# Router logits with the router stationary, routing regrouped, clearing moved to GpSimd, and two stage ends replaced by single waits

## The chip, the cores and the metric

One core of one Trainium2 chip runs the whole program as a single launch. The metric is the device time of one execution in microseconds (us); the number compared is the median of the runs. The engines are TensorE (PE, with its weight loads listed apart as PEld), VectorE (DVE), ScalarE (ACT), GpSimd (POOL) and SyncE (SP), whose queue issues the large transfers.

## What is computed

A trunk of two layers works on 256 latent tokens and 256 context tokens of width 1024. Each layer mixes tokens (attention and a recurrent scan), projects, adds the result, normalises again and applies a channel mixer. The change lies in the second layer, whose channel mixer is a mixture of experts on the 256 latent tokens:

```python
def moe_swiglu(h, router, w1, w3, w2):
    logits = jnp.einsum('bld,de->ble', h, router, preferred_element_type=F32)
    top_v, top_i = lax.top_k(logits, TOP_K)          # TOP_K = 2 of N_EXPERTS = 8
    wts = jax.nn.softmax(top_v, axis=-1)
    gates = jnp.sum(jax.nn.one_hot(top_i, N_EXPERTS, dtype=F32) * wts[..., None], axis=-2)
    y = jnp.zeros_like(h)
    for e in range(N_EXPERTS):
        y = y + gates[..., e:e + 1].astype(h.dtype) * swiglu(h, w1[e], w3[e], w2[e])
    return y
```

## The kernel before

Everything is float32; large products are made from two bf16 parts each (a high part and the rest). Tokens lie in tiles of 128, tiles 2 and 3 being the latent ones; the width is 8 blocks of 128 (`KC`).

**Order of the work.** Every engine has its own program, written out by hand. Engines hand work to one another through semaphores, and at the end of each stage all four compute engines drain and wait for each other (`stage_end`, L394 to L399). The second layer's stages are: mix, levels, states, out (the output projection and the residual add), then one stage with the norm and the routing, one short stage with the first gather, the expert loop, and a last stage that adds the result.

**Norm (L498 to L588).** ACT squares the rows, POOL forms the inverse root, DVE scales the rows into `XN`, PE turns 16 blocks (L583) into PSUM banks, and DVE (L566) and ACT (L535) take them in turn, modulated, into `HT`.

**Routing (L1455 to L1530).** PE computes the logits token-stationary: for each of 2 token tiles and 8 blocks the 128x128 tokens are the weights and the 8 router columns stream (L1458, 16 products, two instructions each as all float32 products here). Then it turns the 16 normalised blocks back into rows (L1463). DVE ranks the 8 logits of each token in a chain of dependent small instructions (L1486 to L1497, ended by the semaphore `r_sel`), computes the gates (L1499 to L1506), waits for PE's five position products (L1469 to L1473), computes positions and the number of rounds (L1509 to L1517), forms the low bf16 part of the rows (L1521, four instructions) behind ACT's high part (L1530), and clears `Y` and `PT` (L1522, L1523). A stage end follows.

**First gather.** PE clears two PSUM banks with products on the zeroed `PT` (L1621, 8 instructions), waits for the one-hot matrix of DVE (L1708), gathers expert 0's tokens (L1605, 32 products); ACT and DVE take them (L1697, L1703). A second stage end follows.

**Experts.** The 24 weight pieces of an expert (16 of 1408 KB, six of 1536 KB, two of 1024 KB) go through a ring of 8 slots. SP issues a piece when its slot is free (L1568, L1580), DVE splits it (L1754), PE multiplies it (L1633 to L1636, L1655). Pieces 0 to 5 of expert 0 are issued ahead, as soon as the states stage is over; pieces 6 and 7 when PE begins the first gather's stage (`pe.sem_inc(S("m_used"), NSLOT - EARLY)`); piece 8 when PE is through with piece 0.

## Time and profile before

| | us |
|---|---|
| median of 3 runs | 1955.58 |
| lowest, highest | 1955.06, 1958.46 |
| span of the profiled execution (the page gives no other time of it) | 1958.8 |
| its stretch from the first turned block of the second layer's second norm to the first weight split | 1225.4 to 1258.0 |
| its stretch from there to the end of the span | 1258.0 to 1958.8 |

The profile has a page of sums and slices, and answers on single stretches: who waited for whom, the chain of work that ended last, instructions in order of time, and the busy share of each engine in a stretch. Times in it are counted from the first instruction. The granted clock is that of TensorE as a share of full speed: 1.00 is 2.4 GHz and 0.50 is 1.2 GHz. A mean duration of a pipelined product includes its overlap with the next; the busy time of a group divided by its count is what one costs in a row.

### The profile page before, as it was taken

How to read it: one execution, taken by the hardware profiler on the slowest of the kernel's cores; microseconds unless marked ns; L12 is line 12 of the kernel's file. 1: busy time of each engine (PE TensorE's matmuls, PEld its weight loads, DVE VectorE, ACT ScalarE, POOL GpSimd, SP SyncE). 2: the span in 40 equal slices, each digit the busy share in tenths (PEclk: the TensorE clock that was granted, in tenths of full speed). 3: DMA queues.
4: the chain of work that ended last, by engine and by line, in shares of the span. 5: the costliest groups of instructions: out<-in, count | busy, mean ns of one | idle time of the engine just before them, and what ended most of it. 6: DMA issues, size and time to landing. Idle time of an engine off the chain costs nothing.

```text
span 1958.8 us, 33901 instructions
## 1 busy us (share of the span) xinstructions
PE 1774.0 (91%) x14848; PEld 1120.0 (57%) x14891; DVE 1169.3 (60%) x1387; ACT 371.3 (19%) x669; POOL 79.2 (4%) x68
## 2 busy tenths in 40 slices
PE   4999999978799999998999966799999998989996
PEld 2334556664344434444556643687786877768683
DVE  2021166874422323223234585699999999999996
ACT  2001055222422212211013323201010010001000
POOL 0032000020000000000230001000000000000000
PEclk9989999999899999999999998699999999999998
DMA  9731200002454544230222105299999999999998
GB/s 332 306 129 65 83 4 25 19 1 86 150 195 179 208 151 178 101 88 20 86 71 80 44 1 220 104 401 407 410 413 412 411 413 409 402 403 413 402 411 349
DMA packets 114969, 420.24 MB, mean 215 GB/s; under 512 B 14008, under 2 KB 20856, under 8 KB 108688
## 3 DMA queue, kind: packets, MB, share of 16 engines
q1 hardware_dynamic: 112784, 417.13, 54.7%
q8 instruction: 118, 1.93, 0.4%
q10 hardware_dynamic: 2048, 1.02, 0.3%
q14 instruction: 19, 0.16, 0.0%
HBM read 417.08 MB, written 1.05 MB: 213 GB/s over the span
## 4 chain that ended last, share of the span: by engine, by line
PE 68%; DVE 17%; DMA 7%; issue 4%; ACT 2%; DVEq 1%; POOL 1%; SPq 0%; POOLq 0%; PEldq 0%; ACTq 0%; PEld 0%
PE PS L1346 11%; PE PS L1655 11%; PE PS L618 10%; DVE ARENA L1754 8%; PE PS L616 8%; PE PS L1306 6%; DMA ARENA<-in_moe_w 6%; PE PS L1241 3%; PE PS L445 2%; PE PS L1633 2%; PE PS L1636 2%; PE PS L1635 2%; PE PS L1134 2%; DVE ARENA L801 1%; DMA ARENA<-in_ada_w 1%
## 5 line engine op out<-in xcount | busy, mean ns | idle before, releaser
L1754 DVE TENSOR_TENSOR ARENA<-ARENA 128x2816 bf16<-128x2816 f32 (+1 forms) x192 | 583.5, 3084 | 19.0 <-DMA ARENA<-in_moe_w 16.7
L1633 PE MATMUL PS<-ARENA 128*128 128x96 bf16 x2816 | 368.2, 207 | 29.9 <-DVE ARENA L1754 26.3
L1636 PE MATMUL PS<-ARENA 128*128 128x96 bf16 x2816 | 367.8, 207 | 2.6 <-issue 2.5
L1635 PE MATMUL PS<-ARENA 128*128 128x96 bf16 x2816 | 367.8, 207 | 0.5 <-issue 0.5
L1633 PEld LDWEIGHTS PS<-ARENA 128*128 128x128 bf16 x2816 | 276.9, 98 | 37.6 <-DVE ARENA L1754 30.1
L1635 PEld LDWEIGHTS PS<-ARENA 128*128 128x128 bf16 x2816 | 277.0, 98 | 9.4 <-issue 8.4
L1636 PEld LDWEIGHTS PS<-ARENA 128*128 128x128 bf16 x2816 | 276.9, 98 | 2.6 <-issue 2.4
L618 PE MATMUL PS<-ARENA 128*128 128x512 f32 (+1 forms) x608 | 243.0, 540 | 0.0
L1655 PE MATMUL PS<-ARENA 128*96 128x512 bf16 x1056 | 237.5, 384 | 2.8 <-DVE ARENA L1754 2.8
L1346 PE MATMUL PS<-ARENA 128*128 128x512 bf16 x1030 | 234.2, 385 | 4.4 <-DVE ARENA L1377 2.8
L378 DVE TENSOR_TENSOR ARENA<-ARENA 128x4096 bf16<-128x4096 f32 (+1 forms) x26 | 91.4, 3522 | 202.1 <-ACT ARENA L372 202.0
L1655 PEld LDWEIGHTS PS<-ARENA 128*96 128x96 bf16 x1056 | 127.9, 122 | 106.2 <-issue 3.9
L1346 PEld LDWEIGHTS PS<-ARENA 128*128 128x128 bf16 x1056 | 103.2, 99 | 139.7 <-issue 20.1
L618 PEld LDWEIGHTS PS<-ARENA 128*128 128x128 f32 x608 | 111.2, 194 | 87.0 <-issue 81.5
L616 PE MATMUL PS<-ARENA 128*128 128x512 f32 (+1 forms) x384 | 156.3, 567 | 0.0
L616 PEld LDWEIGHTS PS<-ARENA 128*128 128x128 f32 x384 | 73.6, 193 | 83.1 <-issue 80.7
L1306 PE MATMUL PS<-ARENA 128*128 128x512 bf16 x517 | 113.5, 379 | 1.5 <-DVE ARENA L1402 0.9
L679 DVE COPY ARENA<-PS 128x512 f32<-128x512 f32 (+1 forms) x24 | 13.4, 558 | 145.7 <-PE PS L618 145.7
L372 ACT ACTIVATE ARENA<-ARENA 128x4096 bf16<-128x4096 f32 (+1 forms) x26 | 74.9, 2888 | 108.3 <-PE PS L1306 68.3
L1306 PEld LDWEIGHTS PS<-ARENA 128*128 128x128 bf16 x528 | 51.6, 98 | 63.5 <-issue 1.4
L1718 ACT ACTIVATE ARENA<-PS 128x384 f32<-128x384 f32 (+1 forms) x48 | 20.7, 464 | 274.5 <-PE PS L1636 274.2
L1241 PE MATMUL PS<-ARENA 128*128 128x512 bf16 x282 | 63.2, 385 | 3.2 <-DVE ARENA L1266 3.0
(224 smaller groups left out, 1603.0 us busy)
## 6 DMA issues: line engine op xcount, KB each, us to landing
ARENA<-in_moe_w SPq DMA_DIRECT2D x136, 1408.0 KB, 16.6
ARENA<-in_moe_w SPq DMA_DIRECT2D x48, 1536.0 KB, 21.0
ARENA<-in_ada_w SPq DMA_DIRECT2D x24, 2048.0 KB, 10.1
ARENA<-in_ffn_w SPq DMA_DIRECT2D x15, 2048.0 KB, 7.9
ARENA<-in_w_in SPq DMA_DIRECT2D x12, 2048.0 KB, 8.0
ARENA<-in_moe_w SPq DMA_DIRECT2D x16, 1024.0 KB, 18.6
ARENA<-in_w_out SPq DMA_DIRECT2D x8, 1024.0 KB, 5.5
ARENA<-in_w_in SPq DMA_DIRECT2D x4, 1024.0 KB, 6.4
```

The costliest lines, as they stand in the source:

```text
L372: act.activation(it["hi"], raw, ACT.Copy).then_inc(S("split_hi"), 1)
L378: dve.tensor_tensor(it["lo"], it["raw"], it["hi"], ALU.subtract).then_inc(S("split_lo"), 1)
L616: mm = pe.matmul(B(bank)[:, part], slot[:, k, P * u:P * u + P], HT[:, k, part], start=k == 0, stop=k == KC - 1)
L618: mm = pe.matmul(B(bank)[:, part], HT[:, k, P * u:P * u + P], slot[:, k, part], start=k == 0, stop=k == KC - 1)
L1241: mm = pe.matmul(B(len(ts) * h + i), a[:, k, P * x:P * x + P], b[:, j, :], start=k == 0 and m == 0, stop=k == KC - 1 and m == 2)
L1306: mm = pe.matmul(B(2 * x + h), a[:, c, P * x:P * x + P], w[:, at:at + 512], start=c == 0 and n == 0, stop=c == FC - 1 and n == 2)
L1346: mm = pe.matmul(B(b0 + i % 3), w[:, k, P * c:P * c + P], x[:, k, :], start=k == 0 and w is hi and x is HTH, stop=k == KC - 1 and w is lo)
L1633: pe.matmul(out, hi[:, f:f + P], HEH[:, k, :], start=k == 0 and b % 4 == 0, stop=False, skip_group_check=True)
L1635: pe.matmul(out, hi[:, f:f + P], HEL[:, k, :], start=False, stop=False, skip_group_check=True)
L1636: mm = pe.matmul(out, lo[:, f:f + P], HEH[:, k, :], start=False, stop=k == KC - 1, skip_group_check=True)
L1655: mm = pe.matmul(B(YBANK + h)[0:SLOTS, :], x, y[:, at:at + 512], start=c == 0 and n == 0, stop=c == FC - 1 and n == 2)
L1754: dve.tensor_tensor(WLO[q % NSLOT][:, 0:n], RAW[q % NSLOT][:, 0:n], WHI[q % NSLOT][:, 0:n], ALU.subtract).then_inc(S("m_lo"), 1)
```

## The change

- The normalised blocks of this norm go to a place of their own (`HTR`), so that slots 6 and 7 of the ring (which lie over `HT`) can be filled early: piece 6 waits for the last product of the output projection, and piece 7 goes out behind it.
- The logits are computed router-stationary: the router's 8 columns are the weights and all 256 tokens stream, 8 products in place of 16, placed between the turned blocks of the norm. The result is 8x256, so DVE copies it and PE turns it twice, back to tokens by experts.
- The rows are turned behind the logits in four groups, each with its own semaphore step, and ACT and DVE take them group by group.
- DVE's chain is reordered: ranking, two low parts, positions of the first round, one-hot, two low parts, other positions, number of rounds, and only then the gates.
- PE gathers as soon as the low parts are done. The clearing of `PT` and `Y` goes from DVE to POOL, at the end of the states stage; PE's zero products (now two, in bf16) stand ahead of the norm's turned blocks.
- The stage ends behind the routing and behind the first gather are gone; the semaphores `m_pt`, `r_rounds` and `m_cleared` are waited for instead.

```diff
+        HTR = A(150, KC, 256)
+        LGT = A(158.5, 256)
...
         def pe_route(pe):
+            def logits(k):
+                pe.wait_ge(S(n + ("ht_act" if k % 2 else "ht_dve")), 24 + k // 2 + 1)
+                return pe.matmul(B(LBANK)[0:N_EXP, 0:256], ROUT[:, k, :], HTR[:, k, :], start=k == 0, stop=k == KC - 1)
+            def rows(x, k):
+                return pe.transpose(B(2 * x + k // 4)[:, P * (k % 4):P * (k % 4) + P], HTR[:, k, P * x:P * x + P], ident)
+            pe.wait_ge(S("m_pt"), 1)
+            zeros = PT.rearrange("p x s -> p (x s)").bitcast(BF16)
+            pe.sem_inc(S("m_used"), USED - 1)
+            for h in range(2):
+                mm = pe.matmul(B(YBANK + h)[0:SLOTS, :], zeros[:, 0:SLOTS], zeros, start=True, stop=True)
+            mm.then_inc(S("m_used"), 1)
+            pe.wait_ge(S(n + "xn"), 14)
+            for k in range(KC):
+                if k >= 4:
+                    logits(k - 4)
+                for x in LAT_TILES:
+                    mm = pe.transpose(B(turn_bank(3, k))[:, P * x:P * x + P], XN[:, x, P * k:P * k + P], ident)
+                mm.then_inc(S(n + "tp"), 1)
+            for k in range(4, KC):
+                mm = logits(k)
+            mm.then_inc(S("r_logits"), 1)
+            for k in range(4):
+                mm = rows(0, k)
+            mm.then_inc(S("r_rows"), 1)
+            pe.wait_ge(S("r_lgt"), 1)
             for x in range(2):
-                for k in range(KC):
-                    mm = pe.matmul(B(0)[:, 8 * x:8 * x + 8], HT[:, k, 256 + P * x:384 + P * x], ROUT[:, k, :],
-                                   start=k == 0, stop=k == KC - 1)
-            mm.then_inc(S("r_logits"), 1)
-            for x in range(2):
-                for k in range(KC):
-                    mm = pe.transpose(B(4 + 2 * x + k // 4)[:, P * (k % 4):P * (k % 4) + P],
-                                      HT[:, k, 256 + P * x:384 + P * x], ident)
-            mm.then_inc(S("r_rows"), 1)
+                mm = pe.transpose(B(LTBANK)[:, 8 * x:8 * x + 8], LGT[0:N_EXP, P * x:P * x + P], ident[0:N_EXP, 0:N_EXP])
+            mm.then_inc(S("r_turned"), 1)
+            for j in range(1, 4):
+                for k in range(4):
+                    mm = rows(j // 2, 4 * (j % 2) + k)
+                mm.then_inc(S("r_rows"), 1)
...
+            pe.wait_ge(S("r_low"), 4)
+            pe_gather(pe, 0)
...
+        def pool_clear(pool):
+            pool.memset(PT, 0.0).then_inc(S("m_pt"), 1)
+            pool.memset(Y, 0.0).then_inc(S("m_cleared"), 1)
...
         def rounds(eng, body):
+            eng.wait_ge(S("r_rounds"), 1)
             n = eng.value_load(NROUND[0:1, 0:1], min_val=1, max_val=NROUNDS)
...
+            elif q == EARLY:
+                sp.wait_ge(S("out_mm"), since(1, "out_mm") + 4)
...
                 for stage in (pool_qk, pool_levels, pool_states):
                     stage(pool, L)
+                    if L == 1 and stage == pool_states:
+                        pool_clear(pool)
                     stage_end(pool, "pool")
```

How the order moves, at three places. In the rows below a name in brackets behind `waits` is the semaphore waited for.

PE from the output projection's last product to the gather, before:

```order
L583 MATMUL PS<-K,ARENA 128x128 [waits pool_stage_done,norm_xn,dve_stage_done,act_stage_done]
L583 MATMUL PS<-K,ARENA 128x128 x7
L1458 MATMUL PS<-ROUT,ARENA 128x8 [waits norm_ht_dve,norm_ht_act]
L1458 MATMUL PS<-ROUT,ARENA 128x8 x15
L1463 MATMUL PS<-K,ARENA 128x128 x16
L1469 MATMUL PS<-ARENA,K 128x8 [waits r_sel]
L1621 MATMUL PS<-BYTES 96x256 [waits pool_stage_done,act_stage_done,dve_stage_done]
L1621 MATMUL PS<-BYTES 96x256 x3
L1605 MATMUL PS<-BYTES,GATE 128x96 [waits m_onehot]
```

The same stretch of PE in the changed kernel:

```order
L1475 MATMUL PS<-BYTES 96x512 [waits m_pt,pool_stage_done,act_stage_done,dve_stage_done]
L1482 MATMUL PS<-K,ARENA 128x128 [waits norm_xn]
L1482 MATMUL PS<-K,ARENA 128x128 x7
L1466 MATMUL PS<-ARENA,ROUT 8x256 [waits norm_ht_dve]
L1482 MATMUL PS<-K,ARENA 128x128 x2
L1466 MATMUL PS<-ARENA,ROUT 8x256 [waits norm_ht_act]
L1469 MATMUL PS<-K,ARENA 128x128 x4
L1492 MATMUL PS<-K,ARENA 128x8 [waits r_lgt]
L1469 MATMUL PS<-K,ARENA 128x128 x12
L1502 MATMUL PS<-ARENA,K 128x8 [waits r_sel]
L1662 MATMUL PS<-BYTES,GATE 128x96 [waits m_onehot,r_low]
```

The zero products went from behind the routing to ahead of the norm, the logits moved in between the turned blocks, and the gather now waits for single semaphores where a stage end stood.

DVE behind the ranking, in the changed kernel (L1522 is the low part, L1758 the one-hot, L1753 the taking of the gathered tokens, L1804 the first weight split):

```order
L1539 TENSOR_TENSOR ARENA<-ARENA 128x16 [waits r_step]
L1522 TENSOR_TENSOR GATE<-PS,GATE 128x512 [waits r_high] x2
L1545 SCALAR_TENSOR_TENSOR ARENA<-PS,ARENA 128x16 [waits r_pos,r_step]
L1758 TENSOR_SCALAR BYTES<-K,POS 128x96 [waits r_step]
L1522 TENSOR_TENSOR GATE<-PS,GATE 128x512 [waits r_high] x2
L1558 CAST NROUND<-BYTES 128x1 [waits r_step]
L1560 TENSOR_SCALAR ARENA<-ARENA 128x2 [waits r_exp]
L1753 TENSOR_TENSOR ARENA<-PS,ARENA 128x384 [waits m_he_hi,r_step]
L1599 TENSOR_LOAD NROUND [waits r_rounds,m_cleared]
L1804 TENSOR_TENSOR ARENA<-ARENA 128x2816 [waits m_raw0]
```

Before, the gates stood ahead of the positions, all four low parts and the two clearings behind the number of rounds, and the one-hot behind a stage end.

SP ahead of the expert loop, before and then in the changed kernel:

```order
L1580 DMA ARENA<-in_moe_w 128x2x1408 [waits m_used] x7
L1587 TENSOR_LOAD NROUND
```

```order
L1636 DMA ARENA<-in_moe_w 128x2x1408 x5
L1636 DMA ARENA<-in_moe_w 128x2x1408 [waits out_mm]
L1636 DMA ARENA<-in_moe_w 128x2x1408
L1644 TENSOR_LOAD NROUND [waits r_rounds]
```

Pieces 6 and 7 no longer wait for PE's first gather; the load of the number of rounds now waits for DVE to have written it.

## Rows read from the trace of the kernel before

**Rows 1.** The page: the span, and the group of weight splits.
```profile
span 1958.8 us, 33901 instructions
...
L1754 DVE TENSOR_TENSOR ARENA<-ARENA 128x2816 bf16<-128x2816 f32 (+1 forms) x192 | 583.5, 3084 | 19.0 <-DMA ARENA<-in_moe_w 16.7
```

**Rows 2.** Stretches: start:end length, busy us (instructions) of each engine, granted clock, DMA share, GB/s.
```profile
1225.30:1229.60 4.30, 3.65 (x16) 3.27 (x16) 2.18 (x4) 2.25 (x4) 0.00 (x0) 0.50 0.00 0
1229.60:1236.70 7.10, 7.04 (x33) 7.04 (x34) 0.00 (x1) 1.29 (x2) 0.00 (x0) 0.50 0.01 2
...
1249.00:1255.00 6.00, 5.96 (x39) 4.68 (x40) 0.79 (x3) 0.49 (x1) 0.00 (x0) 0.50 0.83 295
...
1261.10:1265.30 4.20, 4.16 (x53) 4.16 (x54) 4.20 (x2) 0.18 (x1) 0.00 (x0) 0.50 0.02 4
1265.30:1266.30 1.00, 1.00 (x27) 1.00 (x25) 1.00 (x1) 0.00 (x0) 0.00 (x0) 1.00 0.00 0
...
1290.00:1440.00 150.00, 146.81 (x2140) 114.78 (x2140) 149.38 (x80) 13.11 (x21) 0.00 (x0) 1.00 1.02 409
1440.00:1930.00 490.00, 464.15 (x7101) 371.77 (x7098) 472.70 (x250) 39.66 (x68) 0.00 (x0) 1.00 1.02 409
```

**Rows 3.** SP in order of time: start us, us, instructions; pieces 6 and 7, then 8 and 9.
```profile
1249.01 0.88 SPq L1580 DMA_DIRECT2D ARENA<-in_moe_w  x2
...
1266.23 3.18 SPq L1580 DMA_DIRECT2D ARENA<-in_moe_w  x2
```

**Rows 4.** The chain of waits from the norm to the first split: start us, us, what.
```profile
1225.36 3.66 PE PS L583 x16
...
1229.66 7.00 PE PS L1458 x32
...
1244.70 4.25 DVEq L395
...
1249.04 3.70 PE PS L1621 x8
1252.73 2.52 PE PS L1605 x32
...
1257.99 3.10 DVE ARENA L1754
```

**Rows 5.** POOL, then DVE, in order of time, at the end of the states stage.
```profile
1185.22 1.01 POOL L1020 TENSOR_TENSOR STAT<-STAT,NEGH 128x4 f32<-128x4 f32 x1
...
1186.26 1.12 DVE L1005 SCALAR_TENSOR_TENSOR ARENA<-PS,STAT,ARENA 128x128 f32<-128x128 f32 x4 [1.20 <-POOL STAT L1020]
```

**Rows 6.** DVE in order of time, in the routing and the first gather.
```profile
1236.70 0.17 DVE L1486 COPY ARENA<-PS 128x16 f32<-128x16 f32 x1 [7.54 <-PE PS L1458]
...
1239.38 0.17 DVE L1497 TENSOR_TENSOR ARENA<-ARENA 128x16 f32<-128x16 f32 x1
...
1244.01 2.48 DVE L1521 TENSOR_TENSOR GATE<-PS,GATE 128x512 bf16<-128x512 f32 x4
1246.87 1.76 DVE L1522 MEMSET X<- 128x2048 f32 x1 [0.38 <-issue]
...
1255.80 0.56 DVE L1703 TENSOR_TENSOR ARENA<-PS,ARENA 128x384 bf16<-128x384 f32 x1 [0.59 <-ACT ARENA L1697]
```

**Rows 7.** Prices, by line and shape: busy us, mean ns | idle before.
```profile
L618 PE MATMUL PS<-ARENA 128*128 128x256 f32 x192 | 42.1, 379 | 0.0
L963 PE MATMUL PS<-ARENA 128*128 128x128 f32 x128 | 14.8, 277 | 2.7 <-DVE ARENA L997 2.7
...
L733 POOL TENSOR_TENSOR STAT<-STAT,NEGH 128x64 f32<-128x64 f32 x2 | 21.1, 10549 | 0.2
...
L750 POOL TENSOR_TENSOR ARENA<-ARENA,K 128x512 f32<-128x512 f32 x4 | 5.1, 1270 | 0.0
...
L730 POOL TENSOR_SCALAR STAT<-STAT 128x64 f32<-128x64 f32 x2 | 0.5, 253 | 164.3 <-DVE STAT L710 164.3
L731 POOL TENSOR_SCALAR STAT<-STAT 128x24 f32<-128x24 f32 x2 | 0.4, 217 | 0.2
```

More of the change, by code:

```diff
@@ L1445, in trunk @@
         Y = X[:, 0:2, :]
-        RT = A(16, 9, 2, N_EXP)
-        RV = A(17, 8, 2)
+        RT = A(160.3125, 9, 2, N_EXP)
+        RV = A(160.875, 8, 2)
         NROUNDS = 3
@@ L1467, in pe_route @@
             pe.wait_ge(S("r_sel"), 1)
             one, tri = kc(K_ONE), kc(K_TRI)
-            pe.matmul(B(1)[:, 0:8], tri, RT[:, 8, 0, :], start=True, stop=True)
-            pe.matmul(B(1)[:, 8:16], one, RT[:, 8, 0, :], start=True, stop=False)
-            pe.matmul(B(1)[:, 8:16], tri, RT[:, 8, 1, :], start=False, stop=True)
-            pe.matmul(B(1)[:, 16:24], one, RT[:, 8, 0, :], start=True, stop=False)
-            pe.matmul(B(1)[:, 16:24], one, RT[:, 8, 1, :], start=False, stop=True).then_inc(S("r_pos"), 1)
+            pos = B(LBANK)
@@ new lines, in pe_route @@
+            pe.matmul(pos[:, 0:8], tri, RT[:, 8, 0, :], start=True, stop=True)
+            pe.matmul(pos[:, 8:16], tri, RT[:, 8, 1, :], start=True, stop=False)
+            pe.matmul(pos[:, 8:16], one, RT[:, 8, 0, :], start=False, stop=True).then_inc(S("r_pos"), 1)
+            pe.matmul(B(LTBANK)[:, 16:24], one, RT[:, 8, 0, :], start=True, stop=False)
+            pe.matmul(B(LTBANK)[:, 16:24], one, RT[:, 8, 1, :], start=False, stop=True).then_inc(S("r_pos"), 1)
+            pe.wait_ge(S("r_low"), 4)
@@ L1497, in dve_route @@
             dve.tensor_tensor(RT[:, 8, :, :], RT[:, 3, :, :], RT[:, 4, :, :], ALU.add).then_inc(S("r_sel"), 1)
+            low_rows(0)
+            low_rows(1)
+            then(dve.memset(POS[:, :, NROUNDS * N_EXP:NIT], -1.0))
+            dve.wait_ge(S("r_pos"), 1)
+            pos = B(LBANK)[:, 0:16].rearrange("p (x e) -> p x e", e=8)
+            then(dve.scalar_tensor_tensor(out=RT[:, 7, :, :], in0=pos, scalar=1.0, in1=RT[:, 8, :, :],
+                                          op0=ALU.add, op1=ALU.mult))
+            for c in range(NROUNDS):
+                then(dve.tensor_scalar(POS[:, :, N_EXP * c:N_EXP * c + N_EXP], RT[:, 7, :, :], -1.0 - SLOTS * c, None, ALU.add))
+                if c == 0:
+                    dve_onehot(dve, 0)
+                    low_rows(2)
+                    low_rows(3)
+            dve.wait_ge(S("r_pos"), 2)
+            then(dve.tensor_reduce(CNT[:, 0:1], B(LTBANK)[:, 16:24], AX.X, ALU.max))
+            then(dve.tensor_scalar(CNT[:, 1:2], CNT[:, 0:1], float(SLOTS), 1.0, ALU.is_gt, ALU.add))
+            then(dve.tensor_scalar(CNT[:, 2:3], CNT[:, 0:1], float(2 * SLOTS), None, ALU.is_gt))
+            then(dve.tensor_tensor(CNT[:, 3:4], CNT[:, 1:2], CNT[:, 2:3], ALU.add))
+            dve.tensor_copy(NROUND[:, :], CNT[:, 3:4]).then_inc(S("r_rounds"), 1)
             dve.wait_ge(S("r_exp"), 1)
@@ L1517, in dve_route, with act_route @@
[L1517 to L1525 removed]
+            dve_tokens(dve, 0)
+            dve.wait_ge(S("m_cleared"), 1)
+        def act_route(act):
+            for j in range(4):
+                act.wait_ge(S("r_rows"), j + 1)
+                act.activation(XLH[:, j // 2, 512 * (j % 2):512 * (j % 2) + 512], B(j),
+                               ACT.Copy).then_inc(S("r_high"), 1)
@@ L1562, in sp_slot_free, with sp_piece @@
                 sp.wait_ge(S("m_used"), USED * i + USED + 3 * (q // 4 - 2) + q % 4 + 1)
-        def sp_piece(sp, i, e, q):
-            sp_slot_free(sp, i, q)
+        def sp_piece(sp, i, e, q, first=False):
+            if not first:
+                sp_slot_free(sp, i, q)
+            elif q == EARLY:
+                sp.wait_ge(S("out_mm"), since(1, "out_mm") + 4)
             if q == 16:
@@ L1585, in sp_moe @@
             for q in range(NSLOT):
-                sp_piece(sp, 0, 0, q)
+                sp_piece(sp, 0, 0, q, first=True)
+            sp.wait_ge(S("r_rounds"), 1)
             n = sp.value_load(NROUND[0:1, 0:1], min_val=1, max_val=NROUNDS)
@@ L1614, in pe_scatter @@
                           stop=True).then_inc(S("m_scattered"), 1)
-        def pe_moe_first(pe):
-            pe.sem_inc(S("m_used"), NSLOT - EARLY)
-            flat = PT.rearrange("p x s -> p (x s)")
-            for h in range(2):
-                for a in (0, 256):
-                    pe.matmul(B(YBANK + h)[0:SLOTS, a:a + 256], PT[:, 0, 0:SLOTS], flat, start=True, stop=True)
-            pe_gather(pe, 0)
         def pe_moe(pe):
@@ L1963, in _ @@
                     pool_norm(pool, 2)
-                stage_end(pool, "pool")
-            for _ in range(3):
+                    stage_end(pool, "pool")
+            for _ in range(2):
                 stage_end(pool, "pool")
```

60 lines of the change are left out of this document (19 added, 41 removed).

## The prediction

> **What bounds the kernel now.** The page comes first: one span, and the group of weight splits of the expert stage, which waited 16.7 us in all for a transfer [rows 1]. The stretches show where: from 1290 to 1440 DVE is busy without a gap, from 1440 to 1930 it loses some time, and in both the transfers take the whole share at 409 GB/s [rows 2]. So the expert stage runs at the pace of its transfers once the lead of the ring is used up. The reader should see that nothing in it is changed: whatever is gained ahead of it moves it as a block. Two events start it: SP's issue of piece 8 at 1266.23, when PE is through with piece 0 [rows 3], and ahead of it DVE's first split at 1257.99 [rows 4], on which the first hangs (a split of 3.1, then 66 products of PE). Pieces 6 and 7 went out at 1249.01 [rows 3]; two pieces of 1.44 MB at 409 GB/s take 7.1 us, so they were there before piece 8's turn, and loading them earlier is worth nothing by itself.
>
> The chain of waits then tells what leads to 1257.99: 16 turned blocks, the logits, the rest of the routing, a wait of 4.25 behind DVE's low parts and clearings, the zero products, the gather [rows 4]. This chain I rebuild. PE stays at a granted clock of 0.50 (1.2 GHz) through all of it up to the gather, though its records fill the 11.4 us from 1225.3 to 1236.7 almost completely [rows 2].
>
> **The change, part by part.** The profiled execution spans 1958.8, 3.2 above the median of 1955.58; only differences are worked out, and they are taken from the median.
>
> *Clearing on POOL, at the end of the states stage.* POOL's last instruction ended at 1186.23 and DVE's last, which ends the stage, at 1187.38 [rows 5]. POOL now clears 256 and 2048 elements in that gap. The trace has no such clearing on POOL. One-input instructions there cost 0.253 for 64 elements and 0.217 for 24 [rows 7], 0.9 ns per element more; two-input ones 1.27 for 512, or 2.48 ns [rows 7]; DVE's own clearing took 1.76 for 2048 [rows 6]. A clearing reads nothing, so I take the one-input slope: 0.4 + 2.0 = 2.4 us. POOL ends at 1188.6, and with 0.15 as an allowance for the drain the stage ends **1.35 us later**. Bounds: no delay if it fits the gap of 1.15, and 4.7 at the two-input rate (5.7 + 0.15 - 1.15). The output projection, norm and routing all stand behind this stage end, so the delay is paid in full.
> The Trainium skill ("GPSIMD Engine Reference", section 3.1) says to use DVE for elementwise work and gives 2.6 cycles per element for the two-input case; an estimate from that page at 1.2 GHz makes 2304 elements 5.0 us, the delay 4.0 and the result 1947.9 instead of 1945.2. The slope of the one-input rows is below that.
>
> *Zero products ahead of the norm.* PE waits there for DVE's scaled rows anyway, some 1.5 us; two bf16 products of 512 columns cost 0.4 to 0.9. Nothing; without that cover, 0.9. Behind the routing they cost 3.70 [rows 4].
>
> *Norm and logits.* Old: 1225.36 to 1236.66, 11.30 us, 16 turned blocks at 0.228 and 32 instructions at 0.219 [rows 4]. New: the same 16, plus 8 products of 256 columns, two instructions each. At the low clock such an instruction costs 0.44 (the first four zero products, 8 instructions, 3.49 from 1249.04 to 1252.53; 3.70 / 8 = 0.46 is the upper bound) [rows 4], so 16 x 0.436 = 7.0: exactly what the logits cost now. At full clock it is 42.1 / 192 = 0.219, and a turned block 14.8 / 128 = 0.116 [rows 7]. So the gain is in the clock. After the first expert products it rose 4.2 us after PE began; at the zero products and gather it had not risen 6.0 us after [rows 2]. I take 5. Then 10.6 us of low-clock work shrink to 5.0 + 2.8, plus 0.2 for the last blocks that DVE and ACT still have to take: 8.0, **3.3 less**. Bounds: 10.6 (clock never rises), 5.4 (full from the start).
>
> *From logits to ranking.* Old: DVE starts at once (1236.70) [rows 6]. New: a copy of 8x256 (0.4, between 0.17 for 16 columns and 0.62 for 512 [rows 6]), two turns of 0.12, a copy, with handovers: **0.9 more** (1.4 at the low clock, where four row blocks stand ahead of the turns). The ranking itself, 1236.70 to 1239.55, stays at 2.85 [rows 6]. It ends 3.3 - 0.9 = 2.4 earlier.
>
> *From ranking to the taken tokens.* Old: 1239.55 to 1256.36, 16.8 us [rows 6]. It held the gates, the wait for all five position products, clearings of 2.03, two waits of all engines, the zero products of 3.70 and the gather at low clock. New on DVE: four low parts 2.48, position of the first round 0.42, one-hot 0.45, other positions 0.42, number of rounds 0.97, gates 1.68, the two token parts 1.15, small things 0.15: 7.7. PE is beside it: positions within 1.3, then the gather 3.6 after the ranking, 2.5 at low clock, and ACT's last part at 6.9 at the latest; DVE gets there at 6.6. So DVE's queue sets this end, **9.1 less**. What is late next is DVE itself: its gates could only be hidden if it had less to do.
>
> *Stage end into the loop.* 1256.36 to 1257.99 was 1.63, mostly the load of the number of rounds and branches; the all-engine wait in it is 0.2. **0.2 less**. What queues behind the new waits: SP's load of the number of rounds needs DVE's write, some 4.9 us after the ranking, long before piece 8; POOL's clearing has been over for more than 50 us.
>
> *Piece 0.* PE idles before it as it does now (5.9 us), so it starts at the low clock again (0.50 up to 1265.3 [rows 2]). Counted at nothing; 66 products at 0.08 throughout would be 0.2 more, at full clock 2.3 less.
>
> Sum: +1.35 - 3.3 + 0.9 - 9.1 - 0.2 = **-10.4**; 1955.58 - 10.4 = **1945.2 us**.
>
> **The rivals.**
> 1. *The clock stays low through the logits.* For: 17 us of nearly unbroken PE records at 0.50 [rows 2], and the new products fill only 8 columns of the array. Against: what ran then were turned blocks and 8-column streams; now 256 columns stream. It costs 2.6 + 0.5 + 0.3: -7.0, 1948.6. The Trainium skill ("TensorE: Matmul & The Clock Gate", part 1) says that sustained matmul activity releases the clock within a few us, whatever is issued; by that rule alone the result is 1945.2, and this rival would have no chance. The trace disagrees with it for the old stage, so it keeps one.
> 2. *Full clock from the norm on.* If the zero products keep the clock that the output projection had: another 2.6 off, 1942.6.
> 3. *POOL clears at the two-input rate.* Another 3.35: 1948.6.
> 4. *Nothing arrives.* The transfers are at 409 GB/s from 1290 on; if they, and not PE's use of piece 0, set the pace from a point that does not move (a slower stream behind an earlier start), the gain drains away: 1955.6. Against: SP's issue of piece 8 is a wait for PE, and the queue stood empty before it. This is also the case that the change does not do what it says.
> 5. *Slower: POOL holds the states stage.* POOL's slow kind of instruction, the power, takes 10.55 for 64 elements [rows 7], 165 ns each. Nothing in the stage can hide a POOL clearing beyond 1.15 us. The other terms give 11.7, so it decides from a clearing of 12.7 us, 5.5 ns per element; at 9 ns it takes 20.7 and the result is 1955.6 - 11.7 + 19.7 = 1963.6. Against: every POOL row without a power is at 2.5 ns or less.
>
> **How the numbers follow.** Forecast 0.62; rival 1 0.16; rival 2 0.05; rival 3 0.08; rival 4 0.06; rival 5 0.03. The measurement tells 0.2% (3.9 us) from no change. Faster: 0.62 + 0.16 + 0.05 + 0.08 = 0.91; same 0.06; slower 0.03. Low end: rival 2 without POOL's delay and with one us from piece 0, 1942.6 - 1.35 - 1.0 = 1940.3, so 1940.5. High end: 1948.6 plus 1.9 for half of the other's cost or a spread like that of the three runs: 1950.5.
>
> **What would show it.** POOL's two clearings 2.4 us together and the next stage's first PE instruction 1.3 later behind DVE's last; the granted clock at 1.00 before the logits end; logits instructions near 0.22 at their end; first norm block to ranking's end 11.8 us (14.2 before); ranking to first split 9.2 (18.4 before); first split to piece 8's issue still 8.2; DMA share about 1.0 from there, and that distance to the end of the span unchanged (692.6). The prediction is wrong if the clock is 0.50 at the ranking, if POOL's clearings are above 4 us, if DVE stands waiting between the one-hot and the gates, or if the stretch from piece 8's issue to the end grows.

## The result, and the profile after

The changed kernel takes **1945.18 us**, median of 13 runs (1940.32 to 1955.53), beside 1958.46 for the kernel before in the same measurement (13 runs, 1953.24 to 1966.64). The ratio is 0.994, with an interval from 0.9923 to 0.9957: 8.4 to 15.1 us less (the two medians lie 13.3 apart). The forecast was 1945.2 and 10.4 less.

The page, with the span and the group of weight splits that answer to [rows 1]:

```profile
span 1950.0 us, 33844 instructions
...
L1804 DVE TENSOR_TENSOR ARENA<-ARENA 128x2816 bf16<-128x2816 f32 (+1 forms) x192 | 583.3, 3085 | 17.1 <-DMA ARENA<-in_moe_w 15.5
```

The splits wait 15.5 us for transfers, 16.7 before. The expert stage has kept its shape. Its stretches, and those of the logits and of piece 0 (columns as in [rows 2]):

```profile
1229.50:1233.10 3.60, 3.59 (x13) 2.07 (x14) 1.09 (x3) 1.13 (x2) 0.00 (x0) 0.50 0.86 361
1233.50:1237.60 4.10, 4.10 (x20) 1.47 (x19) 0.68 (x2) 1.13 (x2) 0.00 (x0) 1.00 0.00 0
...
1250.00:1257.00 7.00, 4.35 (x55) 4.35 (x56) 7.00 (x3) 2.28 (x3) 0.00 (x0) 0.50 0.00 0
1282.00:1432.00 150.00, 145.61 (x2131) 114.35 (x2128) 149.86 (x81) 13.16 (x22) 0.00 (x0) 1.00 1.02 408
1432.00:1922.00 490.00, 467.83 (x7093) 376.42 (x7090) 473.42 (x252) 39.46 (x68) 0.00 (x0) 0.99 1.02 409
```

The granted clock is 0.50 (1.2 GHz) up to 1233.2, so for two of the sixteen logits instructions and the start of the third, and 1.00 (2.4 GHz) for the rest; in [rows 2] it was 0.50 for all of them. The chain of waits, which answers to [rows 4]:

```profile
1229.51 1.97 PE PS L1482 x8
...
1235.82 1.82 PE PS L1466 x8
1237.64 0.58 PE PS L1469 x4
1238.23 0.23 PE PS L1492 x2
1238.48 0.19 DVE ARENA L1528
...
1241.34 0.95 DVE GATE L1522 x2
...
1248.11 0.55 DVEq L1599
...
1249.50 3.10 DVE ARENA L1804
```

L1482 is a turned block of the norm, L1466 the logits, L1469 turned row blocks that stand on PE ahead of the two turns of the logits (L1492), L1528 the copy that starts the ranking, L1522 the low parts, L1599 the load of the number of rounds, L1804 the first split. The last logits instructions take 0.23 each (1.82 / 8). The waits of all engines and the 4.25 behind DVE are out of the chain; from the low parts to the loop every piece of it is DVE's.

SP in order of time, to be read against [rows 3]: pieces 6 and 7 now leave in the output projection, piece 8 as before behind piece 0.

```profile
1224.00 0.88 SPq L1636 DMA_DIRECT2D ARENA<-in_moe_w  x2
...
1257.87 7.76 SPq L1636 DMA_DIRECT2D ARENA<-in_moe_w  x3
```

At the end of the states stage (see [rows 5]) POOL clears behind its last power, while DVE ends the stage's own work and PE waits:

```profile
1188.28 0.31 POOL L1581 MEMSET BYTES<- 128x256 f32 x1
1188.53 1.80 POOL L1582 MEMSET X<- 128x2048 f32 x1
...
1188.36 1.13 DVE L1011 SCALAR_TENSOR_TENSOR ARENA<-PS,STAT,ARENA 128x128 f32<-128x128 f32 x4 [1.20 <-POOL STAT L1026]
...
1190.54 1.94 PE L1237 MATMUL PS<-K,ARENA 128*128 128x128 f32 x8 [4.77 <-POOLq L397]
```

To see where the time went, each trace is cut at eight marks. Five are start times of instructions; the first, the ranking's end and the last are ends. They are: the end of DVE's last instruction of the states; PE's first instruction of the output stage; the norm's first turned block; the copy that starts the ranking; the ranking's end; the first split; piece 8's issue; the end of the span. All numbers in us.

| kernel | states to PE | output | norm, logits | ranking | to first split | sum | to piece 8 | piece 8 to end | first split to end |
|---|---|---|---|---|---|---|---|---|---|
| before | 0.13 | 37.85 | 11.34 | 2.85 | 18.44 | **70.61** | 8.24 | 692.57 | 700.81 |
| changed | 1.05 | 38.97 | 8.97 | 2.86 | 8.16 | **60.01** | 8.37 | 692.13 | 700.50 |
| e1 late pieces | 1.05 | 38.97 | 8.98 | 2.85 | 8.17 | 60.02 | 8.36 | 692.44 | 700.80 |
| e2 block delay | 1.05 | 38.96 | 8.97 | 2.86 | 22.11 | 73.95 | 8.22 | 692.01 | 700.23 |
| e3 token logits | 1.06 | 38.97 | 9.92 | 2.85 | 7.96 | 60.76 | 8.02 | 690.47 | 698.49 |
| e4 stage ends | 1.06 | 38.96 | 8.97 | 2.85 | 11.80 | 63.64 | 8.26 | 691.51 | 699.77 |
| e5 POOL early | 0.13 | 37.69 | 9.93 | 2.86 | 8.17 | 58.78 | 8.79 | 690.12 | 698.91 |
| e6 warm | 1.06 | 38.95 | 7.40 | 2.85 | 7.64 | 57.90 | 6.31 | 693.95 | 700.26 |
| e7 POOL gates | 1.05 | 38.95 | 8.97 | 2.85 | 8.20 | 60.02 | 8.34 | 691.49 | 699.83 |
| e8 all | 0.12 | 37.71 | 7.41 | 2.85 | 8.16 | 56.25 | 6.31 | 693.81 | 700.12 |
| e9 gates first | 1.06 | 38.94 | 8.97 | 2.85 | 10.77 | 62.59 | 8.74 | 690.66 | 699.40 |
| e10 Y on DVE | 0.13 | 37.62 | 9.89 | 2.86 | 9.79 | 60.29 | 8.14 | 690.99 | 699.13 |
| e11 PE late | 1.05 | 38.97 | 7.40 | 2.88 | 7.60 | 57.90 | 17.56 | 691.65 | 709.21 |
| e12 best | 0.13 | 37.70 | 7.41 | 2.85 | 6.99 | 55.08 | 6.31 | 692.31 | 698.62 |

Between the first two rows lies the result: 10.60 us up to the first split and 0.31 behind it. The two spans differ by 8.8 only, because in the changed kernel's profiled execution the states ended 2.1 us later (1189.49 instead of 1187.38), in work that the change does not touch. That mark varies from 1182.53 to 1193.85 over these fourteen executions; cuts behind it that no edit touches repeat to a few hundredths up to the first split. So up to there the cuts carry what the times, which vary by several us from run to run, cannot separate. Behind the first split it is otherwise: leaving out e11, the last column runs from 698.49 to 700.81, by more than most edits are worth, so a difference of under 2 us there says nothing.

### The profile page after: what moved, and what is told of

Read it like the earlier page. It is cut to its first block, busy times and chain, and to the rows that moved or that the text cites. A ratio compares the mean times of both kernels' runs of the same rounds, so it can differ in the third digit from the quotient of the medians.

```text
span 1950.0 us, 33844 instructions
## 1 busy us (share of the span) xinstructions
PE 1773.8 (91%) x14828; PEld 1115.8 (57%) x14871; DVE 1167.5 (60%) x1386; ACT 371.2 (19%) x669; POOL 81.2 (4%) x70
## 3 DMA queue, kind: packets, MB, share of 16 engines
q10 hardware_dynamic: 2048, 1.02, 0.2%
HBM read 417.08 MB, written 1.05 MB: 214 GB/s over the span
## 4 chain that ended last, share of the span: by engine, by line
PE 72%; DVE 14%; DMA 7%; issue 3%; ACT 2%; DVEq 1%; POOL 1%; POOLq 0%; SPq 0%; PEldq 0%; ACTq 0%; PEld 0%
PE PS L1704 12%; PE PS L1352 11%; PE PS L624 10%; PE PS L622 8%; PE PS L1312 6%; DMA ARENA<-in_moe_w 5%; DVE ARENA L1804 5%; PE PS L1247 3%; PE PS L1682 3%; PE PS L1685 3%; PE PS L1684 3%; PE PS L447 2%; PE PS L1140 2%; DVE ARENA L807 1%; DMA ARENA<-in_ada_w 1%
## 5 line engine op out<-in xcount | busy, mean ns | idle before, releaser
L1804 DVE TENSOR_TENSOR ARENA<-ARENA 128x2816 bf16<-128x2816 f32 (+1 forms) x192 | 583.3, 3085 | 17.1 <-DMA ARENA<-in_moe_w 15.5
L1682 PE MATMUL PS<-ARENA 128*128 128x96 bf16 x2816 | 372.8, 209 | 23.4 <-DVE ARENA L1804 21.3
L1684 PE MATMUL PS<-ARENA 128*128 128x96 bf16 x2816 | 372.5, 208 | 4.0 <-issue 4.0
L1685 PE MATMUL PS<-ARENA 128*128 128x96 bf16 x2816 | 372.5, 208 | 3.5 <-issue 3.5
```

The lines of the kernel that those rows point to most:

```text
L1682: pe.matmul(out, hi[:, f:f + P], HEH[:, k, :], start=k == 0 and b % 4 == 0, stop=False, skip_group_check=True)
L1684: pe.matmul(out, hi[:, f:f + P], HEL[:, k, :], start=False, stop=False, skip_group_check=True)
L1685: mm = pe.matmul(out, lo[:, f:f + P], HEH[:, k, :], start=False, stop=k == KC - 1, skip_group_check=True)
L1804: dve.tensor_tensor(WLO[q % NSLOT][:, 0:n], RAW[q % NSLOT][:, 0:n], WHI[q % NSLOT][:, 0:n], ALU.subtract).then_inc(S("m_lo"), 1)
```

## The experiments

Ratios are against the kernel before, measured with the runs in question; the changed kernel's is 0.994 [0.9923, 0.9957]. By these intervals only e2 and e11 are clear of the changed kernel. What is said of the others rests on the cuts of one profiled execution each.

**e1, e2: what carries the gain to the end.** e1 holds pieces 6 and 7 back until the low parts are written. e2 delays the whole expert stage on DVE.

```diff
             elif q == EARLY:
-                sp.wait_ge(S("out_mm"), since(1, "out_mm") + 4)
+                sp.wait_ge(S("r_low"), 4)
```

```diff
             dve.wait_ge(S("m_cleared"), 1)
+            for j in range(6):
+                dve.memset(Y, 0.0).then_inc(S("y_again"), 1)
+                dve.wait_ge(S("y_again"), j + 1)
```

> The changed kernel, but pieces 6 and 7 are issued only when the four low parts are done, some 20 us later than in the change and near the place they had before. Theory (the chain to the first split is all; the pieces' early loading is worth nothing): first split, issue of piece 8 and span as in the changed kernel within 0.5 us, time 0.994 of before. Rival (part of the gain is the early loading of two pieces, 7 us of transfers): up to 7 us slower than the changed kernel, DVE waiting for a transfer at the split of piece 6.

> The changed kernel with six more clearings of Y on DVE, one after the other, between the taken tokens and the first split: 6 x 1.8 = 10.8 us. Theory (the expert stage moves as a block): first split and issue of piece 8 10.8 later, distance from piece 8's issue to the end of the span unchanged at 692, time 10.8 us above the changed kernel and so about 0.999 of before. Rival (the transfers or PE absorb a later or earlier start): less than half of it shows, under 5 us, and the distance to the end shrinks by the rest.

e1: 1947.57, 0.9942 [0.9923, 0.9962]. Pieces 6 and 7 left at 1243.48 instead of 1224.00, and every cut is that of the changed kernel within 0.01, but for 0.3 at the end. So loading them early is worth nothing.

e2: 1964.85, 1.0037 [1.0022, 1.0052]. The stretch to the first split grew by 13.95, not by six clearings of 1.76 (10.56), since each of them starts 0.49 behind the end of the one before. By the edit each waits on a semaphore for the one before, and all write the same place; no run tells which of the two makes the gap.

```profile
1252.14 1.76 DVE L1570 MEMSET X<- 128x2048 f32 x1 [0.49 <-DVE X L1570]
```

From the first split to the end it took 700.23, 700.50 in the changed kernel. So the stage moves as a block, by the delay to 0.3 us; nothing of it drains away. That is against the fourth rival of the prediction. The times put e2 some 19 us above the changed kernel; the 5 us beyond the cuts lie ahead of the first mark or in the spread of the times (1940.32 to 1955.53 for the changed kernel), and are not explained.

**e3: is it the shape of the logits that lets the clock rise?** The logits go back to 8-column streams, one for each half of the tokens; the copy, the two turns and their handovers go.

```diff
-                return pe.matmul(B(LBANK)[0:N_EXP, 0:256], ROUT[:, k, :], HTR[:, k, :], start=k == 0, stop=k == KC - 1)
+                for x in range(2):
+                    mm = pe.matmul(B(LBANK + x)[:, 0:8], HTR[:, k, P * x:P * x + P], ROUT[:, k, :], start=k == 0, stop=k == KC - 1)
+                return mm
...
-            then(dve.tensor_copy(lg, B(LTBANK)[:, 0:16].rearrange("p (x e) -> p x e", e=8)))
+            then(dve.tensor_copy(lg, PS[:, LBANK:LBANK + 2, 0:8]))
```

> The changed kernel with the logits token-stationary as before (16 products of 8 columns, same place between the turned blocks), and so without the copy and the two turns. Theory (8-column streams do not bring the clock up, 256-column streams do): granted clock 0.50 from the norm to the ranking, first turned block to the ranking's start 11.3 instead of 8.97 in the changed kernel, to the ranking's end 14.2 instead of 11.8; 2.3 us slower. Rival (the clock would have come up anyway, since the zero products and turned blocks start it): clock 1.00 from about 5 us in, logits at half price, ranking's end at 11.0 or earlier, 0.8 us faster than the changed kernel.

1946.76, 0.9941 [0.992, 0.9961]. The stretches:

```profile
1226.10:1243.00 16.90, 14.87 (x70) 14.05 (x70) 7.05 (x22) 4.63 (x10) 0.89 (x2) 0.50 0.37 155
1243.10:1246.50 3.40, 1.61 (x27) 1.52 (x28) 2.79 (x13) 1.58 (x3) 0.00 (x0) 1.00 0.00 0
```

The clock stayed at 0.50 through 16.9 us in which PE's records fill 14.87, as theory said; with 256-column streams it was up at 1233.2. It rose here at 1243.1, when the turned row blocks were over; why just then no run shows. But the price is small: norm and logits took 9.92, only 0.95 more than in the changed kernel, where 2.3 were expected. The old 11.34 had the same number of turned blocks and 8-column instructions, but the logits stood behind all turned blocks, and here they stand between them. So of the 2.37 that this stretch gained, 1.42 are there without the wide streams. About half of the 1.42 can be seen in the trace before, where PE stood 0.66 waiting for ACT's last block ahead of the logits, and in e3 it does not stand at all. First the kernel before, then e3:

```profile
1229.66 7.00 PE L1458 MATMUL PS<-ROUT,ARENA 128*128 128x8 f32 x32 [0.66 <-ACT ARENA L535]
```

```profile
1230.94 0.86 PE L1467 MATMUL PS<-ROUT,ARENA 128*128 128x8 f32 x4
1231.66 0.67 PE L1484 MATMUL PS<-K,ARENA 128*128 128x128 f32 x2
1232.12 0.86 PE L1467 MATMUL PS<-ROUT,ARENA 128*128 128x8 f32 x4
...
1235.64 3.42 PE L1467 MATMUL PS<-ROUT,ARENA 128*128 128x8 f32 x16
```

The rest, 0.76, is shorter work of PE on as many instructions (9.92 busy, 10.68 before). Most of it lies where the two kinds alternate. Four logits instructions and two turned blocks take 1.18 there (1230.94 to 1232.12), four times over; at the prices of the kernel before (0.219 and 0.228) they would be 1.33. In a row they cost nearly what they did, 3.42 / 16 = 0.21. e3 also writes the two halves of the tokens in turn into two PSUM banks, but it does so in the row as well, so that can be worth little. That leaves the order as the cause, by the trace; no run tests it alone. The other 0.95 come with the wide streams, net of the copy and the turns.

**e4, e9: what the waits and the order are worth.** e4 (the first diff) puts the two waits of all engines back, around the gather. e9 (the second) moves the gates, eight instructions with their wait for the exponential, ahead of the low parts.

```diff
             pe.wait_ge(S("r_low"), 4)
+            stage_end(pe, "pe")
             pe_gather(pe, 0)
+            stage_end(pe, "pe")
...
+            stage_end(dve, "dve")
             dve_tokens(dve, 0)
             dve.wait_ge(S("m_cleared"), 1)
+            stage_end(dve, "dve")
...
+            stage_end(act, "act")
             act_tokens(act, 0)
+            stage_end(act, "act")
...
-            for _ in range(2):
+            for _ in range(4):
                 stage_end(pool, "pool")
```

```diff
+            dve.wait_ge(S("r_exp"), 1)
+            then(dve.tensor_scalar(RV[:, 6, :], RV[:, 5, :], 1.0, None, ALU.add))
...
+                then(dve.tensor_tensor(GT[:, :, N_EXP * c:N_EXP * c + N_EXP], RT[:, 5, :, :], RT[:, 6, :, :], ALU.add))
             low_rows(0)
...
-            dve.wait_ge(S("r_exp"), 1)
-            then(dve.tensor_scalar(RV[:, 6, :], RV[:, 5, :], 1.0, None, ALU.add))
...
-                then(dve.tensor_tensor(GT[:, :, N_EXP * c:N_EXP * c + N_EXP], RT[:, 5, :, :], RT[:, 6, :, :], ALU.add))
             dve_tokens(dve, 0)
```

> The changed kernel with its two stage ends put back: one ahead of the gather (all engines, behind DVE's gates), one behind the taken tokens. Theory (the gain of this part lies in the work that no longer stands in one row: gather beside the gates): the gather starts some 2.9 later (behind the gates), then 2.7 gather at low clock, the token parts, 0.3 for the stage end and the full 1.6 into the loop: ranking's end to first split 8.2 + 3.2 + 0.7 = 12.1, 3.9 us slower than the changed kernel. Rival (the all-engine waits themselves are cheap and nothing is exposed): under 1 us slower.

> Edit: the gates (eight small instructions on DVE, 1.9 us in the changed kernel) stand ahead of the low parts and positions instead of behind them. Theory (DVE's queue alone sets the end of this stretch only as long as the low parts come first; what PE and ACT do hides behind the gates): the low parts, the gather and ACT's last part all come 1.9 later, so the stretch from the ranking's end to the first split grows from 8.16 to about 10.0; the share of the gain that comes from this order is 1.9. Rival (the order does not matter, since DVE does the same work in all): 8.16. From the first split to piece 8 and to the end: unchanged.

e4: 1952.95, 0.997 [0.9954, 0.9987]; to the first split 11.80, which is 3.64 more. PE's gather in order of time:

```profile
1248.69 2.72 PE L1668 MATMUL PS<-BYTES,GATE 128*128 128x96 bf16 x32 [4.92 <-DVEq L397]
```

It waits for DVE's gates instead of standing beside them, and DVE then stands idle 2.34 until ACT's first token part is there, time that its gates filled. The two waits account for a third of the 10.28 that this stretch gained (18.44 to 8.16). Of the rest, the clearing of Y is 1.63 by e10 below; that the zero products (3.70 in [rows 4]) are most of what remains is read from the trace before, and no run put them back.

e9: 1954.74 in a single run; to the first split 10.77, which is 2.61 more where 1.84 was expected. DVE's own rows say why:

```profile
1243.69 0.17 DVE L1541 TENSOR_SCALAR ARENA<-ARENA 128x2 f32<-128x2 f32 x1 [0.85 <-ACT ARENA L1576]
...
1250.83 0.56 DVE L1753 TENSOR_TENSOR ARENA<-PS,ARENA 128x384 bf16<-128x384 f32 x1 [0.83 <-ACT ARENA L1747]
```

So early, the gates wait 0.85 for ACT's exponential, and at the end the gather (2.74 at the low clock) and ACT's two parts are late instead of DVE. The order of the low parts matters by 2.6 us.

**e5, e10: what clearing on POOL costs.** e5 (the first diff) clears ahead of the states stage. e10 (the second) leaves Y's clearing on DVE, behind the gates.

```diff
                 for stage in (pool_qk, pool_levels, pool_states):
-                    stage(pool, L)
                     if L == 1 and stage == pool_states:
                         pool_clear(pool)
+                    stage(pool, L)
```

```diff
+            dve.memset(Y, 0.0).then_inc(S("m_cleared"), 1)
             dve_tokens(dve, 0)
...
             pool.memset(PT, 0.0).then_inc(S("m_pt"), 1)
-            pool.memset(Y, 0.0).then_inc(S("m_cleared"), 1)
```

> The changed kernel with POOL's two clearings ahead of its work of the states stage, where POOL stands idle. Theory (the clearings hold the stage end of the states by 0.9 us): DVE's last instruction of the stage to PE's first of the next 0.13 instead of 1.05, 0.9 us faster than the changed kernel. Rival (the stage end waits for something else, or the clearing disturbs DVE's work when it runs earlier): no gain, or DVE's instructions of the states stage longer.

> Edit: the clearing of Y (2048 elements) stays on DVE, behind the gates; POOL clears the token table alone, 256 elements, at the end of the states stage. Theory (what POOL's 1.80 costs is its 0.92 at the stage end and some 1.1 more in the output stage, since PE's longer pause sends its clock down for longer): DVE's last of the states to PE's first 0.13, the output stage to the first turned block 37.7 to 37.9, so about 2.0 back; the first split 1.8 later behind the ranking; net -0.2 to +0.2 to the first split. If the clock comes up later against the norm, as it did with POOL's clearing ahead of the stage, 0.9 more. Rival (only the 0.92 comes back): net +0.9 to the first split.

e5: 1948.44, 0.9934 [0.9912, 0.9955]. e10: 1947.54, 0.9941 [0.992, 0.9961]. In both the 0.92 of the stage end are back, and besides 1.28 and 1.35 of the output stage. Neither the prediction nor the expectation of e5 had these; that of e10, written after e5, had them. The states end at almost the same moment in the changed kernel and in e10 (1189.49 and 1189.18), so the same window can be compared. First the changed kernel, by stretches:

```profile
1202.00:1205.00 3.00, 3.00 (x8) 1.03 (x7) 0.00 (x0) 0.00 (x0) 0.00 (x0) 0.50 1.04 425
```

Then e10:

```profile
1202.00:1205.00 3.00, 3.00 (x15) 1.37 (x14) 0.00 (x0) 0.00 (x0) 0.00 (x0) 1.00 1.01 413
```

Behind the longer pause PE's clock came back at 1205.9 instead of 1201.9, and in those 4 us it issued half as much (11 products, 20 in e10). This holds beyond these two executions: in the five kernels with 0.13 at the stage end the clock came back 12.6 to 12.9 us behind PE's first instruction of the output stage, in the nine with 1.05 it was 15.3. But the clock then also came up later against the norm (5.8 us behind its first turned block in e5, 3.7 in the changed kernel), which cost 0.96 (e5) and 0.92 (e10) in norm and logits. Net to the first split: e5 gains 1.23. e10 loses 0.28: keeping Y on DVE costs 1.63 there and saves 1.35 elsewhere. **Moving the large clearing to POOL, as the change does, is worth 0.3 us** up to the first split; at the head of the states stage it would be worth 1.5. It costs nothing there: from PE's first instruction of the states stage to its end e5 took 21.68 (1168.53 to 1190.21) and the changed kernel 21.69 (1167.80 to 1189.49).

**e6, e11: the clock and piece 8.** e6 adds products on zeros (16 at the output projection's end, 4 ahead of the norm, 8 ahead of the gather, 20 behind it). e11 has FILL at 80, 80 products behind the gather, so PE comes late to piece 0 while DVE does not.

```diff
+            if L == 1:
+                pe.wait_ge(S("m_pt"), 1)
+                zeros = MOLD[:, 0:1024].bitcast(BF16)
+                for _ in range(16):
+                    pe.matmul(B(7)[0:SLOTS, :], zeros[:, 0:SLOTS], zeros, start=True, stop=True)
...
             pe_gather(pe, 0)
+            for _ in range(FILL):
+                pe.matmul(B(3)[0:SLOTS, :], zeros[:, 0:SLOTS], zeros, start=True, stop=True)
...
+        FILL = 20
```

> The changed kernel with products on the zeroed PT that compute nothing, in three gaps of PE: 16 behind the output projection, 4 behind the two zero products, 8 ahead of the gather, 20 behind it. Theory (the clock falls in PE's gaps, and the low clock is paid on the chain): granted clock 1.00 from the output projection through the logits, first turned block to ranking's end 9.7 instead of 11.8; the gather at 1.4 instead of 2.7, which gives nothing because DVE's gates end it; first split to piece 8's issue 6.2 instead of 8.4; together 4.2 us faster than the changed kernel. Rival 1 (products on zeros do not hold the clock): no change of either stretch. Rival 2 (the expert stage's start is set by DVE's splits and not by PE's first piece): only the 2.1 of the norm shows in the span.

> Edit: as the run with products on zeros that keep PE's clock up, but with 80 of them behind the gather instead of 20 (17 us at full clock), so PE comes to piece 0 some 8 to 9 us after it could, while DVE makes its first splits as early as before; piece 8 goes out by so much later. Theory (the expert stage hangs on DVE's split sequence, and PE's use of piece 0 only has to free the buffer before the ring's lead is used up): from the first split to piece 8 about 15 to 17 instead of 6.3, and from the first split to the end of the span 700 to 702, so the time is that of the run with 20. Rival, the prediction's reading (the issue of piece 8 sets the end, at a fixed distance of 692 to 694): first split to the end 708 to 710, the time 8 to 9 us longer.

e6: 1948.07, 0.9932 [0.9909, 0.9956]. Once up, the clock did not fall again before the loop, the logits gained 1.57 and the way from the ranking to the first split 0.52. A stretch, and then PE's gather in order of time:

```profile
1226.00:1240.00 14.00, 11.88 (x69) 6.65 (x69) 7.83 (x26) 5.80 (x10) 0.41 (x1) 1.00 0.39 160
```

```profile
1241.79 1.53 PE L1674 MATMUL PS<-BYTES,GATE 128*128 128x96 bf16 x32 [0.29 <-DVE GATE L1533]
```

PE also went through piece 0 at the high clock and piece 8 left 2.06 earlier behind the first split. None of this last gain reached the end: piece 8 to end grew by 1.8. So 4.2 us were expected of e6, and by the cuts it is 2.1 ahead at the first split and 2.4 at the end.

e11: 1954.43, 0.9979 [0.9961, 0.9996]. The theory that the stage hangs on DVE's first split alone fell. PE's products on zeros and SP's piece 8, in order of time, and then the waits of DVE from the routing on (us in total, times, longest):

```profile
1239.03 17.43 PE L1519 MATMUL PS<-BYTES 128*96 128x512 bf16 x80
...
1259.45 7.76 SPq L1648 DMA_DIRECT2D ARENA<-in_moe_w  x3
```

```profile
DVE ARENA L1816 <- DMA ARENA<-in_moe_w: 23.0, 47, 2.7
```

DVE split as early as in e6 (57.90 behind the states), piece 8 left 17.56 behind the first split, and the end followed it at 691.65. DVE waited 23.0 for transfers, 16.4 in e6. Over the ten kernels in which piece 8 leaves 8.0 to 8.8 behind the first split it is 691.4 from there to the end on the mean (690.1 to 692.6); with 17.6, 691.65; but with 6.31 it is 693.4 (three kernels, 692.3 to 694.0). So a late piece 8 sets the end, as the prediction had it. (e11 holds back PE's own work on piece 0 together with piece 8's issue; that it is the transfers and not PE rests on DVE's longer waits for them.) At 6.31 the mean is 2.0 longer, which suggests that there something that hangs on the first split takes over. But the two groups touch (692.3 and 692.6) and nothing was measured between 6.31 and 8.0, so this is likely, not shown; and so is that it would be DVE, busy 149.86 of 150 us in the first stretch of the stage.

**e7, e8, e12: towards a better version.** e7 (the first diff, shown without POOL's eight steps and without their removal from DVE) computes the gates on POOL. e8 joins e5, e6 and e7. e12 adds six products on zeros ahead of PE's wait for the ranking.

```diff
             dve.wait_ge(S("m_cleared"), 1)
+            dve.wait_ge(S("g_done"), 8)
...
+            pool_gates(pool)
             for _ in range(2):
                 stage_end(pool, "pool")
```

```diff
+            for _ in range(6):
+                pe.matmul(B(YBANK)[0:SLOTS, :], zeros[:, 0:SLOTS], zeros, start=True, stop=True)
             pe.wait_ge(S("r_sel"), 1)
```

> The changed kernel with the gates computed by POOL (as a power of -0.5, squared, in place of the reciprocal) beside DVE. Theory (DVE's queue sets the end of this part, with the gather at the low clock close behind it): DVE loses 1.7 us of work, then waits for ACT's second part; its token parts end at most 0.1 us earlier, as the gather at low clock and ACT end 0.6 before DVE does now; no more than 0.2 us faster. Rival (DVE's queue alone is the bound): 1.6 us faster.

> POOL's clearings early, the zero products in PE's gaps, and the gates on POOL together. Theory: 0.9 + 4.2 from the two alone, and now the gather at full clock lets the gates' move show, 1.4 more: 6.5 us faster than the changed kernel, about 0.9905 of before. Rival (one of the three is only moved to another engine's wait): the sum stays at or below 5.

> Edit: POOL's clearing ahead of the states stage, products on zeros that hold PE's clock (six of them now also in front of the wait for the ranking, where the clock fell in the combined run), gates on POOL. Theory: the clock stays at 1.00 through the gather, the gather takes 1.5 instead of 2.7, and with the gates off DVE's queue the stretch from the ranking's end to the first split is about 6.9 instead of 8.16; end of the states to the first split about 55 (60.0 in the changed kernel, 56.25 in the combined run), from there to the end 700, ratio 0.992 or below. Rival (the clock falls in it again, whatever runs on zeros): 56.3, and 0.993 as the combined run.

e7: 1944.64, 0.9918 [0.9899, 0.9938], but by the cuts nothing: 8.20 to the first split. What DVE waited for between the ranking and the loop, which was nothing in the changed kernel:

```profile
DVE ARENA L1767 <- ACT ARENA L1761: 1.5, 2, 0.8
```

The 1.6 us that DVE no longer spends on gates, it waits for the gather at the low clock and ACT's two parts. PE and DVE are nearly level there: relieving DVE alone gives nothing.

e8: 1946.24, 0.9933 [0.9912, 0.9953]; first split at 56.25, which is 3.8 ahead of the changed kernel where 6.5 were expected in all. The clock fell once more, at 1233.0, just for the gather (2.64). e12 holds it; PE in order of time:

```profile
1245.28 1.53 PE L1690 MATMUL PS<-BYTES,GATE 128*128 128x96 bf16 x32 [0.28 <-DVE GATE L1535]
```

The gather takes 1.53, DVE waits 0.2, the first split comes at 55.08, as expected. From the ranking's end to it are 6.99: 1.17 less than in the changed kernel, where the gates on POOL alone gave nothing (e7) and the clock alone 0.52 (e6). e12: 1946.09 (6 runs), 0.9922 [0.9894, 0.995]. By the cuts it is 4.9 us ahead of the changed kernel at the first split and 6.8 at the end, of which 1.9 lie in a part that wanders by as much between equal kernels; the times alone, 0.9922 and 0.994, do not tell the two apart.

## Why the prediction was right

By the cuts 10.6 us were gained up to the first split and 10.9 up to the end, where 10.4 were forecast. Three terms of the sum were off (by +0.7, -0.5 and -0.5), and that they cancelled is luck. It is luck, too, that the time itself came out at the forecast 1945.2: the kernel before measured 1958.46 beside it, 2.9 above the median from which the forecast started, and the medians fell by 13.3.

None of the four signs that would have shown the prediction wrong came: the clock was 1.00 at the ranking, the clearings took 2.05, DVE did not wait between the one-hot and the gates, and the way from piece 8 to the end did not grow.

- **What bounds the kernel.** Right: the expert stage follows the work ahead of it as a block (e2), a late piece 8 sets the end (e11), early pieces are worth nothing (e1). What the prediction did not see is how near the other limit is (e6).
- **Clearing on POOL, +1.35.** The clearings took 2.05 together, 2.4 forecast, the stage end came 0.92 later. The one-input slope of [rows 7] was the right choice: 1.80 for 2048 elements is 0.88 ns each. The Trainium skill ("GPSIMD Engine Reference", section 3.1) led to an estimate of 5.0 us; its rate is for two inputs, and the measured clearing decides against using it here. The step that failed is "so the delay is paid in full" as the whole of the bill: PE's longer pause cost another 1.12 in the output stage. The term was 2.04, not 1.35.
- **Zero products, 0.** Right; 1.06 us at 1228.04, while DVE was still scaling the rows.
- **Norm and logits, -3.3.** 8.1 where 8.0 was forecast, by the clock's rise: 3.7 us in, 5 forecast. But the shares were not as forecast. By its bound for a clock that never rises (10.6) the prediction gave 0.7 to the new order and 2.6 to the clock ("So the gain is in the clock"). Of the 3.2 that came, 1.4 are there in e3 at the low clock (9.92 up to the ranking, 11.34 before); the wide streams and their clock bring 1.8 and give 0.84 of it back in the next term.
- **Copy and turns, +0.9.** 0.84 from the logits' end (1237.64) to the copy that starts the ranking (1238.48).
- **Ranking to the taken tokens, -9.1.** 7.24 where 7.7 was forecast. Right in its mechanism: DVE's queue runs through without a wait. Three of its reasons are shown, the two waits of all engines (e4), the order of the gates (e9) and the clearing of Y (e10); the zero products are not tested. But PE and ACT stand only just behind DVE (e7): "its gates could only be hidden if it had less to do" missed the gather at the low clock.
- **Stage end into the loop, -0.2.** Mis-sized: 0.92 where 1.43 was forecast. The load of the number of rounds (0.55) now begins beside the last token part, since no drain stands ahead of it: 0.7 less than before.
- **Piece 0, 0.** Right: clock 0.50 up to 1257.1, 8.37 from first split to piece 8, 8.2 forecast.

Of the rivals, the first (clock low) did not occur. e3 has the low clock, but with the narrow streams and without the copy and the turns, and costs 0.75 to the first split; what the wide streams cost at the low clock throughout, priced at 3.4, no run shows. The second (full clock from the norm on) did not occur by itself: the clock fell at 1226.3, before the two zero products began (1228.04). In e6, which has more of them and 16 already at the output projection's end, it holds, at -1.57 where 2.6 was forecast. The third and the fifth fell with the clearings' 2.05, the fourth with e2.

The Trainium skill ("TensorE: Matmul & The Clock Gate", part 1) says that sustained activity releases the clock within a few us whatever is issued. In the changed kernel the trace agrees (up 3.7 us behind the norm's first block); in e3 it does not: 14.87 us of records in 16.9 us at 0.50.

## What to carry to other kernels

Find the marks on which the long stage behind really hangs, and cut every trace there: cuts repeated to hundredths where times varied by several us, and showed that a move "to an idle engine" was worth 0.3 us, not the 1.8 of its instruction. Price a delay at a stage end with what the pause does to PE's clock in the next stage, not with its length alone. Where two engines are nearly level, relieve both in one version: one alone gave 0 (e7) or 0.52 us (e6), both together 1.17 (e12).

## What the hardware showed beyond expectation

- With a pause that was 0.92 us longer PE's clock came back 15.3 us behind the stage's first product instead of 12.6 to 12.9 (nine kernels beside five), and the output stage took 1.1 to 1.35 more. All nine have POOL's clearing in that place; no run lengthened the pause by other means.
- Products on zeros held the clock at 1.00 through norm, ranking and gather in e6, and in e12, with six more ahead of the wait for the ranking, also in the one gap where it had fallen in e8. Products on zeros cost 0.22 each at that clock (17.43 us for 80).
- Turned blocks and 8-column streams did not bring the clock up in 16.9 us (e3); with 256-column streams between the same blocks it was up 3.7 us behind the first block (changed kernel).
- A DVE clearing of 2048 elements that waits on a semaphore for one of the same place starts 0.49 behind its end (e2).
